# A two-layer decoder trunk on one core: the down projection's k tiles in slabs of 2, 2 and 4, every product added by VectorE into the residual

## The reference

```python
def swiglu(h, w_gu, w_down):
    gate, up = jnp.split(h @ w_gu, 2, axis=-1)
    return (jax.nn.silu(gate) * up) @ w_down
...
        xp = xp + swiglu(rms_norm(xp, norm_ffn[i]), ffn_w_gu[i], ffn_w_down[i])
```

## Time and profile before

| what | value |
|---|---|
| time of the kernel before | 2560.38 us median of 3 runs (2559.22 to 2563.18) |
| span of the profiled execution | 2557.4 us |
| median less span | 3.0 us |
| TensorE busy | 2471.2 us, 97% of the span |
| VectorE busy | 1817.6 us, 71% |
| ScalarE busy | 1147.4 us, 45% |
| folded down projection, layer 0 | from about 1254 us to 1429 us of the span |
| folded down projection, layer 1 | from about 2293 us to 2467 us |

### The profile page before, as it was taken

How to read it: one execution, slowest core, us unless ns; L and a number is a source line. 1 busy time by engine, 2 the same in 40 slices (tenths; PEclk the granted TensorE clock), 3 DMA queues, 4 the chain that set the end, 5 groups by cost and what they waited for, 6 DMA issues and landing times. The chain is left out here.

```text
span 2557.4 us, 49533 instructions
## 1 busy us (share of the span) xinstructions
PE 2471.2 (97%) x19032; PEld 2356.7 (92%) x19032; DVE 1817.6 (71%) x3364; ACT 1147.4 (45%) x1965; POOL 107.8 (4%) x135
## 2 busy tenths in 40 slices
PE   7899988899999999999999999989999999999998
PEld 7799955577899999999999999989999999999998
DVE  6667767777557888886667676764788888666752
ACT  5567577686534433332322353553444333323221
POOL 1310033200000000000000000000000000000000
PEclk9899999999999999999999999999999999999999
DMA  6312389820022343433785323235134434359622
GB/s 211 88 51 77 112 332 370 341 84 1 27 93 69 137 145 136 145 137 101 259 284 201 120 69 110 69 85 171 59 133 140 145 139 153 117 180 327 238 79 83
DMA packets 276591, 371.91 MB, mean 145 GB/s; under 512 B 22152, under 2 KB 215946, under 8 KB 268237
## 3 DMA queue, kind: packets, MB, share of 16 engines
q1 hardware_dynamic: 264573, 294.23, 34.0%
q0 software_dynamic: 11776, 75.50, 7.9%
q10 hardware_dynamic: 80, 0.02, 0.0%
HBM read 271.07 MB, written 98.63 MB: 145 GB/s over the span
## 5 line engine op out<-in xcount | busy, mean ns | idle before, releaser
L1578 PE MATMUL ffn_acc<-trunk_x_ahead,trunk_w_hi 128*128 128x272 f32 x2464 | 470.5, 290 | 1.0 <-PEq L87 1.0
L1578 PE MATMUL ffn_acc<-ffn_x_later,ffn_w_hi_more 128*128 128x272 f32 x2112 | 396.4, 287 | 1.0 <-DVE trunk_xT L1209 0.6
L1578 PEld LDWEIGHTS ffn_acc<-trunk_x_ahead,trunk_w_hi 128*128 128x128 f32 x2464 | 389.4, 190 | 1.1 <-issue 1.1
L1578 PE MATMUL ffn_acc<-trunk_x_ahead,trunk_w_lo 128*128 128x272 f32 x1232 | 356.3, 289 | 0.0
L1578 PEld LDWEIGHTS ffn_acc<-ffn_x_later,ffn_w_hi_more 128*128 128x128 f32 x2112 | 330.9, 188 | 1.4 <-issue 1.4
L1578 PE MATMUL ffn_acc<-ffn_x_later,ffn_w_lo_more 128*128 128x272 f32 x1056 | 304.1, 288 | 0.0
L1578 PEld LDWEIGHTS ffn_acc<-trunk_x_ahead,trunk_w_lo 128*128 128x128 f32 x1232 | 234.0, 190 | 0.0
L1578 PEld LDWEIGHTS ffn_acc<-ffn_x_later,ffn_w_lo_more 128*128 128x128 f32 x1056 | 199.0, 188 | 0.0
L1631 PE MATMUL ffn_acc<-trunk_x_ahead,trunk_w_hi 128*128 128x272 f32 x896 | 171.3, 288 | 1.9 <-issue 1.7
L1451 DVE TENSOR_TENSOR trunk_xT<-ffn_acc,trunk_xT 128x544 f32<-128x544 f32 x136 | 98.2, 722 | 99.6 <-PE ffn_acc L1631 99.5
L935 ACT ACTIVATE ffn_w_hi_more<-trunk_w_raw 128x512 fp32r<-128x512 f32 x132 | 83.3, 631 | 163.2 <-PE ffn_acc L1578 157.7
(11 more groups left out here) (531 smaller groups left out, 6079.6 us busy)
## 6 DMA issues: line engine op xcount, KB each, us to landing
o_kept<-trunk_xT SPq DMA_DIRECT2D x96, 544.0 KB, 4.6
trunk_w_raw<-in_ffn_w_gu SPq DMA_DIRECT2D x88, 512.0 KB, 3.9
trunk_x_ahead<-o_kept SPq DMA_DIRECT2D x56, 544.0 KB, 7.1
ffn_x_later<-o_kept SPq DMA_DIRECT2D x56, 544.0 KB, 8.3
x_saved<-trunk_xT SPq DMA_DIRECT2D x24, 544.0 KB, 2.7
trunk_w_raw<-in_ffn_w_down SPq DMA_DIRECT2D x48, 192.0 KB, 4.6
o_kept<-trunk_xT SPq DMA_DIRECT2D x32, 272.0 KB, 4.9
ffn_x_back<-x_saved SPq DMA_DIRECT2D x16, 544.0 KB, 6.1
```

The lines of the kernel that those rows point to most:

```text
L1578: last = nc.tensor.matmul(bank(2 * PAIR[p] + c)[:, 0:QC], w[:, k * P:(k + 1) * P], x(p, k)[:, c * QC:(c + 1) * QC], start=FRESH[p] and k = ...
```

## The change

1. The slabs hold 2, 2 and 4 pairs instead of 2, 3 and 3.
2. ScalarE copies no products. All 7 products of all 12 sets are added by VectorE.
3. The residual is read straight into `xT`, two tiles for each output pair, before the first product of that pair is added (`load_x`; the first three tiles already during the gate part). `load_back`, `add_back` and the buffer `x_back` go.
4. VectorE's list of a set is put in another order: `d_sum1` and `d_sum3` of the next set stand directly behind the addition of product 0, `d_sum2` and `d_sum4` behind that of product 1.
5. The second slab's operand tiles (m = 2, 3) are all loaded during the first. Of the third slab, m = 4, 5 are loaded during the second, and m = 6, 7 in set 7 as their places come free; in set 8 TensorE waits for the latter only in the middle of each product.
6. All six flat activation tiles are loaded during the last set.

```diff
-FOLDED_SLABS = ((0, 2), (2, 3), (5, 3))
+FOLDED_SLABS = ((0, 2), (2, 2), (4, 4))
...
+            load_x(2)
+            slab1, parts1 = [(i, m) for i in DOWN for m in (2, 3)], (0, 3, 8, 13, 14)
+            slab2, parts2 = [(i, m) for i in DOWN for m in (4, 5)], (0, 5, 10, 14, 14)
             for z in range(SETS):
-                if z and z + 1 < SETS and z not in (4, 8):
+                if z and z + 1 < SETS and z != 2 * OUTS:
                     load_raw0(z + 1)
                 if z and z + 2 < SETS:
                     load_raw1(z + 2)
+                if z == 1:
+                    load_x(1)
+                    sp.wait_ge(act_stored, 32 * NFLAT)
+                    load_x(5)
+                if z == 2:
+                    sp.wait_ge(d_lo_ready, d_count(1, D_22))
+                    load_x(0)
+                    load_x(4)
...
             def d_add(z, n):
                 dve.wait_ge(d_products, PRODUCTS * z + n + 1)
...
-            finish(LAST, b21, b22, ())
+            finish(LAST, b21, b22, (), lambda: d_add(0, 0))
...
                 d_low(z, D_22)
                 d_low(z, D_S4)
-                if adds:
+                if z:
                     d_add(z, 0)
+                if more:
+                    d_sum1(z + 1)
+                    d_sum3(z + 1)
                 d_add(z, 1)
-                if adds:
-                    d_add(z, 2)
-                if not adds:
-                    d_add(z, 4)
+                if more:
+                    d_sum2(z + 1)
+                    d_sum4(z + 1)
+                d_add(z, 2)
                 if more:
                     d_low(z + 1, D_1)
...
+                    if z == 2 * OUTS and k == 2:
+                        pe.wait_ge(op_loaded[1][i], 64 * shares(i))
```

More of the change, by code:

```diff
@@ L845, in _ @@
             load_raw1(1)
+            for tile in (3, 7, 6):
+                load_x(tile)
             with sp.Fori(FLAT + 2, LAST) as r:
@@ L1234, in scale_s0, with finish @@
                 nc.vector.tensor_tensor(g0[:, :], g0[:, :], rows[:, 0:H2], ALU.mult).then_inc(s0_scaled, 1)
-            def finish(n, left, right, free):
+            def finish(n, left, right, free, between=None):
                 dve.wait_ge(s1_ready, n + 1)
@@ L1242, in finish @@
                     dve.wait_ge(sem, count)
+                if between is not None:
+                    between()
                 nc.vector.tensor_tensor(right, g1, c22, ALU.mult).then_inc(act_ready, 1)
@@ L1501, in _ @@
                     flat_low(0)
-                if adds:
-                    d_add(z, 3)
-                if more:
-                    d_sum1(z + 1)
-                    d_sum3(z + 1)
-                    d_sum2(z + 1)
-                    d_sum4(z + 1)
-                else:
-                    act_low(2)
-                if adds:
-                    d_add(z, 4)
-                if backs:
-                    add_back(z, 0)
+                d_add(z, 3)
                 if more:
@@ L1523, in _ @@
                 else:
+                    act_low(2)
+                d_add(z, 5)
+                if not more:
+                    act_low(3)
                     flat_low(1)
-                if adds:
-                    d_add(z, 6)
-                if backs:
-                    add_back(z, 1)
-                if z in (9, 10):
-                    act_low(z - 9)
+                d_add(z, 6)
             act_low(4)
@@ L1610, in folded @@
                 pe.wait_ge(d_lo_ready, d_count(z, DOWN_NEEDS[n]))
[L1611 removed]
                 m0, count = pairs_of(z)
[L1613 to L1614 removed]
+                if z == 0:
+                    pe.wait_ge(op_loaded[0][i], 32)
+                elif z == OUTS:
+                    pe.wait_ge(op_loaded[1][i], 32 * shares(i))
+                elif z == 2 * OUTS:
+                    pe.wait_ge(op_loaded[0][i], 64)
                 if n in (0, 1, 3):
```

132 lines of the change are left out of this document (42 added, 90 removed).

## The result

| | median | span of runs |
|---|---|---|
| before | 2561.64 us (5 runs) | 2559.22 to 2565.33 |
| after | 2575.58 us (5 runs) | 2573.55 to 2585.25 |

What follows compares the result with a forecast made beforehand. TensorE, busy 97% of the span, bounds the kernel: 19.4 us of new waits less 12.1 us gone, plus 3.4 us of clock, is +10.7 us on 2560.4, so 2571 us; eight-in-ten range 2558 to 2581 us.

Steps and rivals of the forecast that it cites:

- Set 0: VectorE stands at `d_sum3(1)` for late upper weights, so TensorE idles before product 4: 5.1 us layer 0, 3.7 us layer 1.
- Sets 1 to 3: Late upper weights delay product 4: no wait in set 1, 2.0 us in set 2, 1.5 us in set 3, each layer.
- Sets 4 to 7: Set 4's wait goes whole (3.4 + 3.1 us); no new wait until set 7, 1.5 us there, each layer.
- Set 8: Operand tiles of m = 6 and 7 arrive mid-product; 0.3 us kept per layer of the earlier 3.0 and 2.3 us.
- It just holds: Set 8: tile supply for products 1, 3, 5 at 13.2, 20.3, 26.1 us against need at 15, 21, 27.
- The clock: Granted clock falls to 1.2 GHz behind each layer's set 0 wait, 1.7 us each, +3.4 us.
- new waits: TensorE waits added in the folded parts of both layers: 8.8 + 2 x (2.0 + 1.5 + 1.5 + 0.3) = 19.4 us.
- gone: TensorE's existing waits for weight loads in the folded parts, 6.7 + 5.4 = 12.1 us, counted as removed.
- A: Rival: set 0 as forecast, little wait in sets 2, 3 and 7, no clock fall; -0.9 us, 2559.5 us; chance 0.12.
- B: Rival: VectorE not held in set 0, as upper weights land by about 1260 and 2298; 2553 us; chance 0.07.
- C: Rival: VectorE's additions bound the short sets, waits at every second product; 2585 us and more; chance 0.04.

Runs made afterwards that it cites:

- experiment 3: Changed kernel without the four residual loads of sets 1 and 2: 2559.35 us, ratio 1.0037 to the kernel before.
- experiment 5: Changed kernel with only SyncE's list reordered (upper weights ahead of some operand tiles; in set 7 behind all 14): 2587.14 us, ratio 1.0091 to before.
- experiment 1: Changed kernel with only VectorE's list reordered, next set's sums behind the additions of products 1, 2 and 3: 2550.49 us, ratio 1.0006 to before.
- experiment 2: Changed kernel with the later order of VectorE's sums in set 0 alone: 2566.26 us, ratio 1.0069 to the kernel before.
- experiment 7: Experiment 6 with four more unused copies of 128 x 256 on VectorE in each of sets 1 to 7: 2565.52 us, ratio 1.0014 to before.
- experiment 6: Changed kernel with the edits of experiment 1 and experiment 5 together: 2556.59 us, ratio 0.9984 to the kernel before.
- experiment 8: Experiment 6 with product 4's addition earlier in sets 0 and 7, set 9's upper weights ahead of the last tiles: 2551.54 us, ratio 0.9980 to before.

## Why the prediction was right

**Set 0** (predicted 5.1 and 3.7 us; 3.8 and 4.8 measured). The chain was exact: landing at 1267.0, product 4 at 1269.6, that is the 2.5 + 0.1 us of the prediction. The landings differed. Counted from the beginning of set 0 the upper weights landed at 8.6 and 7.3 us in layers 0 and 1 of before, and at 7.3 and 8.3 in after. So the prediction was 1.3 us too high in one layer and 1.1 too low in the other, and that the sums agree (8.8 predicted, 8.7 measured) is luck. In the traces of experiments 3 and 5, which leave set 0 as it is, the wait was 4.2 to 5.6 us. That the order of the list is the cause is shown by experiment 1.

**Sets 1 to 3** (0, 2.0, 1.5 in each layer; 0.4, 1.2, 2.0 and 0, 2.7, 0 measured). The rule was that product 4 starts at L + 2.6 where L is the landing after the set's beginning, in place of 6.0:

| set, layer 0 | L forecast | L measured | L + 2.6 - 6.0 | measured wait |
|---|---|---|---|---|
| 0 | | 7.3 | 3.9 | 3.8 |
| 2 | 5.4 | 4.6 | 1.2 | 1.2 |
| 3 | 4.9 | 5.4 | 2.0 | 2.0 |

The rule holds to 0.1 us, in set 1 too. The landings were told less well: in set 1 of layer 0 the weights landed 3.9 us into the set where 1.2 was forecast, since the second half took 9.3 us from its issue and not the 4.9 of the earlier trace rows; that is where the 0.4 us come from. In layer 1 they landed at 6.1 us in set 2 and 3.2 in set 3, forecast 5.4 and 4.9, so that one wait of 2.7 us stood where two were forecast (3.5). That the residual loads make the weights of sets 2 and 3 late is shown by experiment 3.

**Sets 4 to 7.** The wait of set 4 went whole, as forecast. Set 7: 1.5 forecast, 2.6 and 2.0 measured; set 5 of layer 1 had 0.9 where none was forecast.

**Set 8** (0.3). None in layer 0, 1.9 us for an operand tile in layer 1. "It just holds" was right for one layer: the tiles of the middle of product 3 have about no slack, as after and experiments 1 to 3, with the same loading, showed (0 to 1.9 us).

**The clock** is the term that was mis-sized: two falls at 1.7 us were forecast, three came, at 2.4, 2.5 and 1.5 us. I had the price from the fall in the earlier trace rows, 3.4 us long after an idle time of 2.6 us; behind the waits of 3.8 and 4.8 us it lasted 6.8 us. And the earlier trace rows said that 2.6 us can be enough, which the wait of 2.7 us then was. The rule of the Trainium skill that the prediction named (TensorE: Matmul & The Clock Gate, HAM oscillation), that a wait for data between stretches of matmuls brings the next stretch to the lower level, held in the three windows above, and not behind the waits of 2.1 us and less of the same trace.

In sum: new waits 22.3 for 19.4 us, gone 12.1 for 12.1, clock 6.4 for 3.4: 16.6 in place of 10.7. The forecast had the right waits in the right places, before product 4 behind `d_sum3`; its size was a third too small, half of that by the clock.

**The rivals.** A (waits cancel): waits of 1.2, 2.0 and 2.7 us were there in sets 2 and 3, and the clock fell. B (faster): the upper weights landed at 1267.0, after VectorE had stood 2.4 us for them. C (VectorE is the bound): no wait before product 2 in any set of the changed kernel, and experiment 1 does all its additions at 1.0006; experiment 7 gives the point from which it comes.

## What to carry to other kernels

Before an instruction is moved up an engine's list, read from the trace when its input lands, and which instruction behind it frees a PSUM bank; the wait of TensorE is then the landing plus the list up to that addition, to 0.1 us here. Where a queue of transfers sets the landing, taking out one wait brings the next reader to its own landing sooner, and the wait moves on (experiment 2): redo the sum for the sets behind. A list on one engine has to be changed with the list that feeds it (experiments 5 and 6). In these traces each of the eleven waits of TensorE of 3.3 us and more in the folded parts had the clock at 1.2 GHz behind it, and three of eight between 2.1 and 3.0 us; the price was about half of the part of the low stretch that lay behind the end of the wait, 1.5 to 2.9 us where the wait was one of the eleven.

## What was not expected of the hardware

- The fall of the clock after one wait of TensorE was not of one length: 6.8 us at 1.2 GHz behind 3.8 and 4.8 us (after) and 5.6 and 4.6 us (experiment 3), 3.4 us behind 2.7 us (after, layer 1), but also behind 4.2 and 4.6 us (experiment 5), and 10.2 us behind 7.5 and 8.4 us (experiment 5). Waits of 2.2, 2.5 and 2.7 us had a fall behind them (experiments 1 and 8, after), and waits of 2.2, 2.6 and 3.0 us none (experiments 7 and 2).
- The upper weights behind the same 14 operand tiles landed at different times in the two layers of one execution, 8.6 and 7.3 us after set 0 began in before, 7.3 and 8.3 in after. No cause was looked for; it is 1.3 us of a wait that is paid in full.
- DMA moved 410 GB/s in the window at 2339.7 us, while VectorE and TensorE were at work, as in the earlier trace rows; this is above the some 358 GB/s that the Trainium skill (DMA: Bandwidth & Descriptors, Where 436 GB/s comes from) gives as one core's limit on the DRAM side. The section gets this figure as half of a stack's 716 GB/s, for two cores, and here one core runs alone; the measurement decides.
